# Moving the squares of the head outputs from GpSimd to ScalarE, and splitting GpSimd's low parts of the output weights, in a hybrid encoder layer

## What is computed

```python
def hybrid_layer(x, ...):
    xn = rms_norm(x, norm1_w)
    hq, hf_f, hf_b, hi, hg, aq, ak, av = split(xn @ w_in)
    o_hg = hgrn2_bidirectional(...)   # 4 heads of 128: o = rms_norm(o_fwd + o_bwd, norm_w) * silu(hg)
    o_da = diff_attention(...)        # 4 heads of 128: o = rms_norm((p0 - lam * p1) @ v, subln_w) * 0.8
    h = x + concatenate([o_hg, o_da]) @ w_out
    return h + expert_choice_moe(rms_norm(h, norm2_w), router_w, w1, w3, w2)
```

## Time and profile before

| what | value |
|---|---|
| median of 3 runs | 2071.4 us |
| the profiled execution | 2072.68 us |
| its span | 2070.9 us |
| granted TensorE clock, mean of the span | 0.99 |
| TensorE, matmuls | 2020.7 us busy, 98% |
| VectorE | 1615.2 us busy, 78% |
| ScalarE | 1339.2 us busy, 65% |
| GpSimd | 93.6 us busy, 5% |

### The profile page before, as it was taken

One profiled execution on the slowest core, in us unless ns is written; L12 is line 12 of the kernel. 1 busy time (PEld: TensorE's weight loads), 2 busy tenths in 40 slices (PEclk: granted clock), 3 DMA queues, 4 the chain that ended last, 5 costly groups with the idle time before them and its releaser, 6 DMA issues.

```text
span 2070.9 us, 27971 instructions
## 1 busy us (share of the span) xinstructions
PE 2020.7 (98%) x10828; PEld 1555.4 (75%) x10828; DVE 1615.2 (78%) x1190; ACT 1339.2 (65%) x1027; POOL 93.6 (5%) x52
## 2 busy tenths in 40 slices
PE   7999999989799999999999999999999999999998
PEld 6899998768577777777777777776777777777776
DVE  5247766764788888888888888888888888888886
ACT  4234433642477777777777777777777777778774
POOL 0000000300100000000000000000000000000000
PEclk9999999989899999999999999999999999999999
DMA  5222224135599999999999999999999999999994
GB/s 168 62 69 80 88 77 168 62 102 184 188 374 364 391 353 396 368 381 377 364 393 362 395 355 388 370 386 372 371 390 357 396 363 395 354 393 367 375 387 154
DMA packets 192388, 618.17 MB, mean 299 GB/s; under 512 B 13680, under 2 KB 38000, under 8 KB 192336
## 3 DMA queue, kind: packets, MB, share of 16 engines
q1 hardware_dynamic: 188640, 604.86, 77.8%
q0 software_dynamic: 3696, 12.59, 2.6%
HBM read 596.96 MB, written 20.45 MB: 298 GB/s over the span
## 4 chain that ended last, share of the span: by engine, by line
PE 94%; DVE 3%; DMA 1%; ACT 1%; issue 0%; POOL 0%; SPq 0%; ACTq 0%; POOLq 0%; DVEq 0%
PE pair L582 29%; PE pair L584 29%; PE pair L583 29%; PE pair L663 2%; PE pair L937 1%; PE pair L736 1%; PE pair L760 1%; PE pair L721 1%; PE pair L884 1%; PE pair L747 0%; DMA x_in<-x 0%; DVE top_tokens L1659 0%; PE pair L703 0%; DVE affinity_t L1660 0%; DMA v_tm<-projected 0%
## 5 line engine op out<-in xcount | busy, mean ns | idle before, releaser
L1738 DVE TENSOR_TENSOR chunk_low<-ring,chunk_high 128x3072 fp32r<-128x3072 f32 x383 | 1178.7, 3087 | 221.0 <-ACT chunk_high L1205 221.0
L1205 ACT ACTIVATE chunk_high<-ring 128x3072 fp32r<-128x3072 f32 (+1 forms) x384 | 980.9, 2563 | 212.6 <-PE pair L584 212.3
L582 PE MATMUL pair<-chunk_high,xe_high 128*96 128x512 f32 (+1 forms) x1536 | 579.2, 377 | 1.4 <-DVE xe_low L1732 1.4
L584 PE MATMUL pair<-chunk_high,xe_low 128*96 128x512 f32 (+1 forms) x1536 | 574.9, 374 | 0.0
L583 PE MATMUL pair<-chunk_low,xe_high 128*96 128x512 f32 (+1 forms) x1536 | 573.2, 373 | 0.0
L582 PEld LDWEIGHTS pair<-chunk_high,xe_high 128*96 128x96 f32 x1536 | 248.1, 162 | 90.2 <-DVE chunk_low L1738 2.6
L584 PEld LDWEIGHTS pair<-chunk_high,xe_low 128*96 128x96 f32 x1536 | 247.8, 161 | 90.2
L583 PEld LDWEIGHTS pair<-chunk_low,xe_high 128*96 128x96 f32 x1536 | 248.4, 162 | 87.3 <-issue 0.3
L582 PE MATMUL pair<-chunk_high,hid_high 128*96 128x512 f32 x704 | 280.3, 398 | 0.0
L584 PE MATMUL pair<-chunk_high,hid_low 128*96 128x512 f32 x704 | 276.8, 393 | 0.0
L583 PE MATMUL pair<-chunk_low,hid_high 128*96 128x512 f32 x704 | 276.2, 392 | 0.0
(11 more groups left out here) (210 smaller groups left out, 1862.4 us busy)
## 6 DMA issues: line engine op xcount, KB each, us to landing
ring<-w SPq DMA_DIRECT2D x288, 1536.0 KB, 9.4
ring<-w SPq DMA_DIRECT2D x96, 1024.0 KB, 8.4
raw_w<-w_in SPq DMA_DIRECT2D x16, 1024.0 KB, 5.4
projected<-stage SPq DMA_DIRECT2D x36, 128.0 KB, 1.7
wo_raw<-w_out SPq DMA_DIRECT2D x8, 512.0 KB, 3.3
x_in<-x SPq DMA_DIRECT2D x6, 512.0 KB, 8.1
queries_and_keys<-qk_raw SPq DMA_DIRECT2D x8, 384.0 KB, 2.9
x_again<-x SPq DMA_DIRECT2D x6, 512.0 KB, 4.7
```

Source lines behind the costliest of these rows:

```text
L582: pe.matmul(dst, a_high, b_high, start=first, stop=False)
L584: return pe.matmul(dst, a_low, b_high, start=False, stop=last)
L1205: act.activation(ch[c % SPLIT][:, 0:n], ring[c % RING][:, 0:n], ACT.Copy).then_inc(ch_done, 1)
L1738: dve.tensor_tensor(cl[c % SPLIT][:, 0:n], ring[c % RING][:, 0:n], ch[c % SPLIT][:, 0:n].bitcast(F32), ALU.subtract).then_inc(cl_done, 1)
```

## The change

ScalarE now makes all squares of the head outputs: the recurrent ones right behind their copy, in the same step, and the attention ones of all tiles. GpSimd keeps the five low parts only, each in four pieces of 256 columns; the last piece of each signals. As VectorE's low parts (tiles 5 to 7) and GpSimd's could otherwise be counted in the wrong order, VectorE's get a semaphore of their own. The root of the first four tiles stays at step 20.

```diff
+WO_PARTS = 4
+    wol_late = sem("wo_low_late_done")
+    def low_part_of(k):
+        return (wol_done, k + 1) if k < WO_EARLY else (wol_late, k - WO_EARLY + 1)
 # SP, load_w_out
-                    sp.wait_ge(wol_done, k - 1)
+                    sp.wait_ge(*low_part_of(k - 2))
 # TensorE, w_out_step
-                pe.wait_ge(wol_done, k + 1)
+                pe.wait_ge(*low_part_of(k))
 # ScalarE
         def evac_gla(i):
             act.wait_ge(go_mm, i + 1)
             act.activation(mixed[:, i, 0:512], GLA, ACT.Copy).then_inc(go_ev, 1)
+            if i >= 1:
+                act.wait_ge(g_red, i)
+            act.wait_ge(go_ev, i + 1)
+            act.activation(sq_o[:, 0:512], mixed[:, i, 0:512], ACT.Square).then_inc(g_sq, 1)
...
         def attention_squares(i):
-            act.wait_ge(o_red, i)
+            if i >= 1:
+                act.wait_ge(o_red, i)
...
                 evac_attention(done)
-                if done >= SAMPLE_TILES - 1:
-                    attention_squares(done)
+                attention_squares(done)
 # VectorE, w_out_low: then_inc(wol_done, 1) becomes then_inc(wol_late, 1)
 # GpSimd: gla_squares and attention_squares are gone, and the loop over a with them
+            for i in range(WO_PARTS):
+                cols = slice(i * D // WO_PARTS, (i + 1) * D // WO_PARTS)
+                ins = pool.tensor_tensor(wol[k][:, cols], wo_raw[k % 2][:, cols], woh[k][:, cols].bitcast(F32), ALU.subtract)
+            ins.then_inc(wol_done, 1)
+
+        for k in range(WO_EARLY):
+            w_out_low(k)
```

More of the change, by code:

```diff
@@ L1552, in w_out_low @@
             dve.wait_ge(woh_done, k + 1)
-            dve.tensor_tensor(wol[k][:, :], wo_raw[k % 2][:, :], woh[k][:, :].bitcast(F32), ALU.subtract).then_inc(wol_done, 1)
+            dve.tensor_tensor(wol[k][:, :], wo_raw[k % 2][:, :], woh[k][:, :].bitcast(F32), ALU.subtract).then_inc(wol_late, 1)
         def attention_reduce(i):
```

## The result

The changed kernel takes 2075.05 us (median of 20 runs, 2072.11 to 2079.17) beside 2072.65 us for the kernel before (20 runs, 2070.45 to 2074.43). The medians are 2.4 us apart. The ratio is 1.0014, 95% interval 1.0008 to 1.0020, which is 2.9 us slower, 1.7 to 4.2. That is under the 0.2% that this kernel's measurement was said to tell apart, and inside the range of 2072.2 to 2080.0. The forecast was 4.2 us slower, 2075.6 as a median.

What follows compares the result with a forecast made beforehand. The prediction took the attention stage as TensorE-bound, with ScalarE's new wait for VectorE's reduction lengthening the path. Late steps and clock summed to 3.2 to 4.4 us, 4.2 taken, giving 2075.6 us; range 2072.2 to 2080.0.

Steps and rivals of the forecast that it cites:

- The bound and the wait that comes along: Attention stage, TensorE-bound: ScalarE's recurrent square inherits GpSimd's 4.63 us wait for VectorE's reduction, making exponentials 3.2 to 7.4 us late.
- One sign: At step 13, ScalarE's square of a recurrent tile was to wait 3 to 4 us for VectorE's reduction.
- the wait of GpSimd: Kernel before: GpSimd waits 4.63 us for VectorE's reduction before squaring the next tile; claimed to cost nothing.
- The stall at step 16: VectorE waited there for both GpSimd squares, delaying step 17's exponentials to 416.92; claimed to go with the squares.
- The rival that nothing takes the stall's place: Attention stage: ScalarE's 1.68 us slack holds everything and the low clock stays away; -3.0 - 1.0, 2067.4 us; chance 0.06.
- The clock term: TensorE's clock around the stall: sum 3.2 us if it never falls, 4.4 if it falls at the 2.3 us idle time.
- The early fall of the clock: Rival: clock falls to 1.2 GHz at step 15's idle 2.2 us, adding 2.7 to 6.9 us, 2078.3 us; chance 0.27.
- Quarters at 0.62 us each, no fixed cost: GpSimd's five low parts of 2.47 us become 20 pieces of 0.62 us each, with no fixed cost per piece.
- The charge of 0.6 us at steps 14 and 15: At each of these steps a GpSimd low-part piece was to hold VectorE's critical softmax factor for 0.6 us.
- The range's upper end: 2080.0 us: the early clock fall, with costlier pieces and a little more.
- All at nothing: GpSimd's order, semaphores, weight loads, the root and its two table loads were claimed to cost nothing.
- Same or slower: Whole-kernel chances: same 0.44, slower 0.52, faster 0.04, with 0.2% (4.1 us) as the bound.

Runs made afterwards that it cites:

- the attention squares: Kernel before with only the attention squares of tiles 0 to 2 moved to ScalarE; recurrent squares and whole low parts stay on GpSimd: ratio 0.9980.
- the two buffers: Changed kernel with a second buffer for the recurrent squares, so tile i's square waits for the reduction of tile i-2: ratio 0.9977 to the kernel before.
- the high part first: Changed kernel with ScalarE's high part of the output weights issued ahead of the recurrent square instead of behind it: ratio 1.0009 to the kernel before.

## Why the prediction held, and where it did not

*The bound and the wait that comes along* held. The exponentials of steps 13 to 17 were expected at 399.9, 405.7, 412.6, 416.95 and 421.45; they start at 399.87, 405.48, 412.55, 416.84 and 421.33, each within 0.22 us. The idle times of TensorE, expected at 1.4, 1.4, 2.2, 0.8 and 2.3 us, are 1.33, 1.21, 2.08, 0.78 and 2.27. Taking the wait away in two different ways turned the loss into a gain; putting it alone into the kernel before made a loss. One sign was a little off: the wait at step 13 is 4.33 us and not 3 to 4. The text also says that the chain is TensorE's own work until 408.9 us; it goes through VectorE and ScalarE from 382.5 to 385.8 us, in both kernels, which changes nothing here. And the wait of GpSimd did not cost nothing everywhere: at step 16 the chain of the earlier trace rows runs from a reduction (412.79) through the recurrent square that waited for it and the attention square queued behind that one.

*The stall at step 16* was worth more than its 2.2 us of two squares. Without it and without a new wait, three squares moved give 4.1 us. The rival that nothing takes the stall's place had -4.0, which the attention squares (-4.1) and the two buffers (-4.8) then showed.

*The clock term* was the one mis-sized. The text took 4.2, close to the 4.4 for a fall at the idle time of 2.3 us, and had 3.2 for a clock that never falls before the root. The profiled execution is that second case, and the output projection starts at 446.13 where 447.8 was stated. The lateness is 4.4 us at the exponentials of step 17, as expected. It is 2.8 at the root, so the steps between give back 1.6 us, with 6.8 us less at the low clock, where the text had 1.3 for this case. Another 0.26 lies in the matmuls before the projection, and 2.54 are left.

*The time came out near for two reasons, and one is luck.* 2075.6 was stated and 2075.05 measured. The forecast of 4.2 us stood on a kernel before of 2071.4 (3 runs), which 20 runs put at 2072.65; the two errors have opposite signs. The groups by clock show a steadier figure: the changed kernel is 3.6 us slower than the one before among executions at 0.991 or lower, and 4.1 among those at 0.992 or higher. Over all executions it is less, since 70 of 106 executions of the kernel before lie in the lower group and only 10 of 31 of the changed kernel. So the longer path costs about 4 us, and a clock that falls less often gives part of it back. The line between the groups was drawn afterwards, so this is a reading of the record and not an experiment.

*The early fall of the clock*, the main rival at 0.27, did not occur in the two profiled executions of the changed kernel. It did in the one with the high part first, after the same 2.08 us of idleness. So neither branch is excluded for a single execution; how often each occurs at that place was not measured.

*Quarters at 0.62 us each, no fixed cost* was wrong by a little. The text compared a subtraction with a square, two different operations. The same operation takes 2.36 us whole and 2.77 in four pieces that no longer wait for VectorE: 0.41 more for three more instructions, so about 0.14 each. The range's upper end counts costlier pieces; no run shows more for them than this. The charge of 0.6 us at steps 14 and 15 came out as 0.39 and 0.52.

*All at nothing* held for loads and the root: ScalarE waits for no weight load from 380 to 430 us (the kernel before had one such wait, of 0.9 us), and the piece of 1.28 us before the root starts 2.8 us later, like the work around it.

*Same or slower*: the time moved the way that was forecast, by less than the 0.2% bound. The text had given that 0.44 and a change above the bound 0.52, so it leaned to the other side.

## What to carry to other kernels

When work moves to another engine, its waits move along, and what is queued behind them there pays. Before moving, write down for each wait in which step of the other engine its releaser is issued; if that is a later step than the waiter's, add a buffer or issue the work a step later, before anything else. Move one kind of work at a time: here one part of the change held the gain and another the loss.

## What was unexpected of the hardware

An idle time of 2.08 us of TensorE left the granted clock at 1.00 in one kernel and was followed by 0.50 in another. 2.27 us left it at 1.00 in the changed kernel and not in the one with whole low parts. So a short idle time is a risk and no rule. What a low clock costs depends on where it lies: 6.8 us less of it behind the root gave 0.2 us in one pair of executions, where ScalarE set the pace, and 1.5 us in another, where the last eight transposes before the output projection went from 1.71 to 0.87 us. Splitting an operation to let another engine in sooner can hold that engine longer: four pieces of 2.78 us in all reached into VectorE's factor (0.74 us instead of 0.22 at step 15), which the whole 2.35 us just missed. Where both start together the split does help (VectorE's difference at step 12, 1.29 us beside pieces, 2.92 beside a whole part).
